# Gate rows one chunk ahead, first query parts in other places, first pair's maxima in two steps

## The reference, cut to what matters

```python
z, xbc, dt_raw, q, k, v, g_ssd, g_att = jnp.split(h @ w_in, ...)
xbc = silu(causal_conv4(xbc) + conv_b)          # xs: 2048 columns, B and C: 4 groups of 128
y_diag = einsum('bclgn,bcsgn', cm, bm) * decay @ (xs * dt)
y_off  = cm @ previous_state * exp(a_cum)       # chunks of 128 positions
y = y_diag + y_off + xs * d_skip
return rms_norm(y * silu(z)) * ssd_norm_g       # by group of 512 columns
```

## Time and profile before

| what | value |
|---|---|
| median of three runs | 2201.11 us |
| the profiled execution | 2201.85 us, its span 2199.8 us |
| PE busy | 2022.4 us (92% of the span) |
| DVE busy | 993.9 us (45%) |
| ACT busy | 702.0 us (32%) |
| POOL busy | 218.5 us (10%) |

### The profile page before, as it was taken

How to read it: one execution, slowest core, us unless ns; L and a number is a source line. 1 busy time by engine, 2 the same in 40 slices (tenths; PEclk the granted TensorE clock), 3 DMA queues, 4 the chain that set the end, 5 groups by cost and what they waited for, 6 DMA issues and landing times.

```text
span 2199.8 us, 23022 instructions
## 1 busy us (share of the span) xinstructions
PE 2022.4 (92%) x9514; PEld 1407.9 (64%) x9514; DVE 993.9 (45%) x1558; ACT 702.0 (32%) x1122; POOL 218.5 (10%) x281
## 2 busy tenths in 40 slices
PE   7999999997999999889999999999995988888887
PEld 6767788896888788777777765666693332332232
DVE  4466524426666522677888436652235111111113
ACT  4343422324444312554555323552121110100100
POOL 2000000002000000001111002110023111111110
PEclk9999999998999999999999999999996999999999
DMA  7331122242222322232222221112229999999995
GB/s 259 106 112 61 67 87 96 97 153 105 97 96 96 134 96 86 100 136 90 74 96 101 87 95 58 58 58 77 77 106 376 414 423 423 424 422 422 417 411 225
DMA packets 56856, 380.43 MB, mean 173 GB/s; under 512 B 12936, under 2 KB 13192, under 8 KB 23856
## 3 DMA queue, kind: packets, MB, share of 16 engines
q1 hardware_dynamic: 38304, 339.23, 39.5%
q0 software_dynamic: 17872, 38.68, 5.0%
q10 hardware_dynamic: 576, 1.05, 0.1%
HBM read 378.82 MB, written 27.89 MB: 185 GB/s over the span
## 4 chain that ended last, share of the span: by engine, by line
PE 70%; DMA 16%; DVE 8%; ACT 3%; issue 1%; POOL 1%; SPq 0%; DVEq 0%; POOLq 0%; ACTq 0%
PE PS L490 17%; PE PS L491 16%; PE PS L492 16%; DMA AR<-in_wexp 15%; PE PS L1071 5%; PE PS L864 4%; PE PS L537 2%; DVE AR L1331 2%; DVE rf L1113 2%; ACT rf L1928 1%; PE PS L845 1%; PE PS L1094 1%; PE PS L486 1%; PE PS L897 1%; PE PS L929 1%
## 5 line engine op out<-in xcount | busy, mean ns | idle before, releaser
L490 PE MATMUL PS<-rf,rf 128*128 128x512 f32 (+1 forms) x1896 | 725.2, 382 | 22.9 <-DVE rf L1113 16.0
L491 PE MATMUL PS<-rf,rf 128*128 128x512 f32 (+1 forms) x1896 | 712.4, 376 | 0.0
L492 PE MATMUL PS<-rf,rf 128*128 128x512 f32 (+1 forms) x1896 | 711.5, 375 | 0.0
L1113 DVE TENSOR_TENSOR rf<-AR,rf 128x1024 fp32r<-128x1024 f32 (+1 forms) x210 | 268.4, 1285 | 385.1 <-ACT rf L1928 384.8
L490 PEld LDWEIGHTS PS<-rf,rf 128*128 128x128 f32 x1896 | 360.1, 190 | 97.6 <-issue 22.7
L492 PEld LDWEIGHTS PS<-rf,rf 128*128 128x128 f32 x1896 | 360.1, 190 | 64.8
L491 PEld LDWEIGHTS PS<-rf,rf 128*128 128x128 f32 x1896 | 360.3, 190 | 64.2 <-issue 3.1
L1928 ACT ACTIVATE rf<-AR 128x1024 fp32r<-128x1024 f32 (+1 forms) x210 | 229.1, 1101 | 304.4 <-PE PS L492 210.1
L1071 PE MATMUL PS<-AR 128*64 128x512 f32 x1024 | 271.7, 639 | 51.9 <-DMA AR<-in_wexp 50.8
L1071 PEld LDWEIGHTS PS<-AR 128*64 128x64 f32 x1024 | 84.2, 147 | 233.6 <-issue 159.8
L1873 DVE TENSOR_TENSOR AR<-AR,PS 128x256 f32<-128x256 f32 x32 | 13.5, 421 | 360.3 <-ACT AR L2370 360.3
(11 more groups left out here) (326 smaller groups left out, 1830.4 us busy)
## 6 DMA issues: line engine op xcount, KB each, us to landing
AR<-in_wexp SPq DMA_DIRECT2D x62, 2048.0 KB, 35.9
AR<-in_wpack SPq DMA_DIRECT2D x123, 1024.0 KB, 5.1
AR<-in_wexp SPq DMA_DIRECT2D x68, 1024.0 KB, 38.1
AR<-acud POOLq DMA_DIRECT2D x16, 512.0 KB, 4.1
AR<-ya SPq DMA_DIRECT2D x4, 1024.0 KB, 7.9
bvec<-bv POOLq DMA_DIRECT2D x1, 2560.0 KB, 16.3
AR<-in_x SPq DMA_DIRECT2D x4, 512.0 KB, 7.4
AR<-bvec POOLq DMA_DIRECT2D x8, 256.0 KB, 3.0
```

The lines of the kernel that those rows point to most:

```text
L490: e.i.matmul(o, ws[0], xs[0], start=start, stop=False)
L491: e.i.matmul(o, ws[0], xs[1], start=False, stop=False)
L492: return e.i.matmul(o, ws[1], xs[0], start=False, stop=stop)
L1113: e.i.tensor_tensor(rounded(p.place + p.width, p.width), src, rounded(p.place, p.width).bitcast(F32), ALU.subtract).then_inc(*tick("w_lo", ...
```

## The change

1. **Gate rows one chunk ahead.** PE computes zt(g, 0) between cbm and `xs_rows(g, 3)`, and zt(g, c + 1) at the head of chunk c; the fourth chunk has none. ACT applies their Silu in the same order. DVE computes XD of chunk 0, then `weigh(g, 0)`, then XD of chunks 1 to 3 (L1493).
2. **Places.** The first two parts of q0 take the places of the last two xs parts, and are split with the fourth group's other parts, between cbm and `xs_rows(3, 3)`, as in the other groups the next xs parts are. The later places of q, kv and of the gates turn with them.
3. **Maxima in two steps.** In the first attention one yield stands between head 0 and head 1, on DVE and on ACT.

```diff
             c.free = emptied(fourth[i - 3])
         else:
-            c.free = emptied(early[i - 2]) if i < 2 else (read_by(thirds[8]),)
+            c.free = emptied(early[i - 2]) if i < 2 else (read_by(thirds[10]),)
...
     for i, p in enumerate(thirds):
-        p.place = WRo + 4096 + 2048 * (i % 4)
-        p.free = (read_by(thirds[i - 4] if i > 3 else zs[-1] if i < 2 else xs[i - 4]),)
+        p.place = WRo + 4096 + 2048 * ((i + 2) % 4)
+        p.free = (read_by(thirds[i - 4] if i > 3 else xs[i - 2] if i < 2 else zs[-1]),)
     gates = [p for c in fourth for p in c.parts if p.key[0][0] == "g"]
     for i, p in enumerate(gates):
-        p.place = WRo + 6144 + 2048 * (i % 3)
-        p.free = (read_by(gates[i - 3] if i > 2 else thirds[9 + i]),)
+        p.place = WRo + 6144 + 2048 * ((i + 1) % 3)
+        p.free = (read_by(gates[i - 3] if i > 2 else thirds[(8, 9, 11)[i]]),)
...
+            def gate_rows(g, c):
+                tc = slice(128 * c, 128 * c + 128)
+                b, was = banks.take(("zt", g, c), ("a_out", ("z", g, c)))
+                e.wait_ge(*at(*was))
+                for k in range(8):
+                    e.wait_ge(*at("w_lo", (f"z{g}", k // 4)))
+                    wh, wl = (cut(w, 4) for w in halves(f"z{g}", k // 4))
+                    m = product(PS[:, b, :], (HH[k][:, tc], HL[k][:, tc]), (wh[:, k % 4, :], wl[:, k % 4, :]),
+                                k == 0, k == 7)
+                m.then_inc(*tick("acc", ("zt", g, c)))
...
                 m.then_inc(*tick("acc", ("cbm", g)))
+                gate_rows(g, 0)
                 xs_rows(g, 3)
                 for c in range(4):
                     eb, tc = EB[:, c % 2, :], slice(128 * c, 128 * c + 128)
...
+                    if c < 3:
+                        gate_rows(g, c + 1)
                     if c:
                         b, was = banks.take(("of", g, c), ("v_out", ("of", g, c)))
...
                 maxima(0)
+                yield
                 maxima(1)
-                yield
                 yield
...
                 if c < 3:
-                    e.wait_ge(*at("v_out", ("xd", g, 3)))
+                    e.wait_ge(*at("v_out", ("xd", g, c)))
...
-                if g < 3:
-                    lows.upto(e, base + 8)
+                lows.upto(e, base + 8)
                 xs_rows(g, 3)
...
                     e.i.tensor_tensor(h8(XD[:, n, :]), h8(XS[:, n, :]), b4(DT, n, g), ALU.mult).then_inc(
                         *tick("v_out", ("xd", g, n)))
-                weigh(g, 0)
+                    if n == 0:
+                        weigh(g, 0)
...
                 exps(0)
+                yield
                 exps(1)
-                yield
                 yield
...
+            def gates(g, c):
+                e.wait_ge(*at("acc", ("zt", g, c)))
+                if c > 1 or g:
+                    e.wait_ge(*at("v_out", ("fn", g, c - 2) if c > 1 else ("fn", g - 1, c + 2)))
+                e.i.activation(ZB[:, c % 2, :], ps(("zt", g, c)), ACT.Silu).then_inc(*tick("a_out", ("z", g, c)))
...
-                if g < 3:
-                    highs.upto(e, base + 8)
+                highs.upto(e, base + 8)
+                gates(g, 0)
                 exponents(g, 0)
                 for c in range(4):
...
                     if c < 3:
+                        gates(g, c + 1)
                         exponents(g, c + 1)
```

## The result

| | before | after |
|---|---|---|
| median of six runs | 2201.03 us | 2209.35 us |
| the profiled execution; its span | 2201.85 us; 2199.8 us | 2208.44 us; 2206.6 us |
| mean granted clock | 0.968 | 0.965 |

The change made the kernel slower: ratio 1.0039, 95% interval 1.0026 to 1.0052, which is 8.3 us by the medians and 6.8 us by the two profiled spans. The prediction, 2202.2 in a range of 2195.6 to 2205.6, is wrong. In the new file most lines around the change are 6 to 7 higher: `turn` is still L790, yd is L851, `finish` on DVE L1450, the sum with yd L1529, XD L1498.

A forecast was written before the change was run, and what follows sets the result against it. The prediction took the loop of DVE, ACT and POOL, not PE, as the bound. Its terms, -1.45 + 0.96 + 3L - (4.85 - L) = -5.34 + 4L with L = 1.6, gave +1.1 us: median 2202.2, range 2195.6 to 2205.6.

The forecast's parts named there:

- What bounds the loop: Group loop: DVE, ACT and POOL follow their own loop; DVE waits for PE only in the fourth chunk, 7.9 us in all.
- Where PE goes and what it meets: Group loop: zt fills the fourth-tile wait, but about 4.8 us of waiting returns at `turn`; three groups cost 0.96 us.
- 5.58 - 0.38 - 0.5: Wait at `turn`: PE's gain of one zt, less the 0.38 us previously spare, less the copy's 0.5 us delay.
- I take L = 1.6: Low clock behind the wait at `turn`: us lost per group on `turn` and yd, bounds 0 to 2.3.
- 0.15: Groups 1 and 2: `turn` starts 0.15 us later, at unchanged clock.
- 5.34: Whole kernel: the fixed terms sum to -5.34 us, to which 4L is added.
- The 2.3 us that the low clock took from q0 are gone, since the low stretch is spent on yd: Start of q0: its wait goes and q0 no longer loses 2.3 us to low clock; part of the gain 4.85 - L.
- Group 3: Last group: two low-half splits and PE's new order put the fourth transposition 3.05 us later; with q0, gain 4.85 - L.
- Maxima: First attention: handling one head first brings mv 1.45 us earlier, bounds 0 and 2.25.
- Other queues: POOL's copy of sums and ACT's Silu and exponentials: covered by DVE's work, costed at 0.
- the low clock lasts as behind q0's wait: Rival, behind the wait at `turn`: L = 2.3 lies wholly on the path, +3.9 us, 2205.0; chance 0.18.

The follow-up runs named there:

- filled: Changed kernel plus 18 matmuls of 128 x 512, results thrown away, in PE's wait ahead of each `turn`; 2195.99 us, ratio 0.9972.
- maxima_only: Kernel before with only the first pair's maxima in two steps; 2200.12 us, ratio 0.9998.
- both_late: Kernel before with moved places, the two q0 splits where DVE idles, and maxima in two steps; 2192.97 us, second run 2195.78 us.
- gate_only: Kernel before with only the gate rows one chunk ahead and XD waited for one chunk at a time; 2216.30 us, ratio 1.0067.
- places_only: Kernel before with only the first q0 parts in the last xs places and their splits one chunk earlier; 2200.26 us, ratio 0.9994.
- split_rows: Changed kernel with yd(g,3) ahead of `turn`, late q0 splits, and two of eight zt(g,3) steps moved ahead of yd(g,3); 2196.58 us, ratio 0.9977.
- places_late: Kernel before with only the moved places, the splits of q0's first two parts standing where DVE idles in group 3; 2194.57 us, ratio 0.9971.
- yd_first: Changed kernel with PE doing yd(g,3) ahead of `turn` in each group's fourth chunk; 2199.22 us, ratio 0.9990.

## Why the prediction was wrong, point by point

- **What bounds the loop** was right. DVE, ACT and POOL set the pace; kernels without low clock behind the fourth chunk's wait stay near 68.2 us a group, whether gate rows are ahead or not. What DVE waits for PE in the fourth chunk, where the prediction had put it, is small: 2.1 us before, 1.9 in filled.
- **Where PE goes and what it meets** was right: four waits of 4.55 us at `turn` (forecast 4.8, though its terms, 5.58 - 0.38 - 0.5, give 4.7), none at the fourth tile.
- **"I take L = 1.6"** is the step that failed. By the group it is 71.46 - 68.25 - 0.15 = 3.06 us, by the spans (6.8 + 5.34) / 4 = 3.03. The 0.15 in it is the forecast's. It lies outside even the stated bounds, 0 to 2.3. Two things were wrong in it. Yd was taken at 1.7 times its length and took 1.85 times (3.52 against 1.90); `turn` and yd together lost 2.0 us. And the low stretch was priced by those of 3.25 to 4.6 us in the earlier trace rows; behind this wait it lasted 7.7 us, so the next tile was slowed as well and ACT and DVE with it, which is the other 1.1 us. Why it lasts so long here is not shown. That 20 small matmuls come first is one difference from the earlier trace rows, but the same instructions do not fix its length: behind the second long wait in the first attention, with the same tile behind it, it was 3.75 us before and 4.67 us in maxima_only, and behind yd(0,0)'s start 5.4 us in both_late and 1.9 in its second run. The bound should have let the stretch be longer than any that was seen. With L = 3.03 the sum gives +6.8, and the forecast is "slower".
- **"The 2.3 us that the low clock took from q0 are gone, since the low stretch is spent on yd"** was wrong as well, for the same reason: the low stretch outlasted yd. The timeline of PE after, the first and the tenth matmul of q0:

```profile
1232.82 0.77 PE L490 MATMUL PS<-rf,rf 128*128 128x512 f32 x1
...
1236.75 0.39 PE L490 MATMUL PS<-rf,rf 128*128 128x512 f32 x1
```

  q0 starts without a wait, and its first nine matmuls take 1236.75 - 1232.82 = 3.93 us, where nine at full clock, 0.23 apart, take 2.1: 1.9 us came back. The table's tail shows it: 435.8 us after, 431.7 in filled. In the sum this stands inside L, which for group 3 is 2.0 (`turn` and yd) + 1.9.
- **Group 3**: the 3.05 us were put on the two splits; the group is (71.56 - 65.90) - (71.46 - 68.24) = 2.4 us longer, with the splits (after) and without (gate_only). The size was near, the cause was not: both are late there, and PE's zt alone is enough.
- **Maxima**: 1.45 forecast, 1.80 measured (119.00 against 120.80); mv waits 1.46 us, forecast about 1.4.
- **Other queues** cost nothing, as forecast: DVE shows no wait for `sums_in` or for the exponentials.
- The rival "the low clock lasts as behind q0's wait" named the right mechanism, its place, and the point from which it decides (a low stretch of more than about 4 us). Its price of 2.3 was still too small.

## What to carry to other kernels

When work moves forward in an in-order queue, its old place becomes a wait, and PE's lower clock level falls on whatever stands behind that wait. Price that work at twice its time, and don't bound the low stretch by the ones that the trace before shows. Where the wait can't be removed, put behind it what nobody waits for: yd ahead of `turn` was worth 10 us of the changed kernel's 2209. And place small jobs of another engine by its idle time: two splits cost 6.7 us ahead of a copy on the path and nothing in the fourth chunk, where the engine was idle.

## What the runs showed of the hardware

- The length of a low stretch, counted from the end of the wait, is not fixed by the length of the wait: 7.7 us behind 4.56 us (changed kernel), 3.75 us behind 4.75 us, 8.9 us behind 3.85 us (places_only). Nor is it fixed by what runs in it: behind 2.7 us, with the same instructions, it was 5.4 us from the start of yd(0,0) in one run of both_late and 1.9 us in the other.
- Nor does the length of a wait alone decide whether the clock falls. The same wait of 1.24 us ahead of yd(1,0) left it at 1.00 in the changed kernel and was followed by 0.50 for 3 us in split_rows; behind 2.27 us it was low in places_late, behind 2.53 us at the same place it stayed at 1.00 in both_late. Behind 2.31 us it fell in every one of yd_first's four groups.
- Eighteen matmuls a group whose result is thrown away made the changed kernel 13 us faster.
